# The differential-attention loop of a two-layer diffusion trunk: scores before transposes, maxima before low parts, exponentials between high parts

## The reference, cut to what matters

```python
def diff_attention(q, k, v, lam, subln_g, lam_init):
    """q (B,H,Tq,2,dk), k (B,H,Tk,2,dk), v (B,H,Tk,dv) -> (B,H,Tq,dv)."""
    scale = DIFF_QK_DIM ** -0.5
    def block(qb):
        s = jnp.einsum('bhqmd,bhkmd->bhmqk', qb, k).astype(F32) * scale
        p = jax.nn.softmax(s, axis=-1)
        a = (p[:, :, 0] - lam * p[:, :, 1]).astype(v.dtype)
        return jnp.einsum('bhqk,bhkd->bhqd', a, v)
    o = map_query_blocks(block, q)
    return rmsnorm(o, subln_g) * (1.0 - lam_init)
```

## Time and profile before

| | before |
|---|---|
| median of 3 runs | 2940.73 us (2940.59 to 2941.97) |
| the profiled execution | 2940.5 us |
| its span, first to last instruction | 2938.6 us |
| busy PE / DVE / ACT / POOL | 98% / 45% / 37% / 21% |
| granted TensorE clock, mean | 0.996 of full speed |

### The profile page before, as it was taken

How to read it: one execution, slowest core, us unless ns; L and a number is a source line. 1 busy time by engine, 2 the same in 40 slices (tenths; PEclk the granted TensorE clock), 3 DMA queues, 4 the chain that set the end, 5 groups by cost and what they waited for, 6 DMA issues and landing times.

```text
span 2938.6 us, 44082 instructions
## 1 busy us (share of the span) xinstructions
PE 2877.4 (98%) x18396; PEld 2756.4 (94%) x18396; DVE 1330.6 (45%) x2291; ACT 1076.5 (37%) x1947; POOL 614.0 (21%) x312
## 2 busy tenths in 40 slices
PE   6999999999999999999999999999999999999998
PEld 5999999999999999999999999999999989899997
DVE  4343443123557575446344434421146567554543
ACT  4333333221444544422343333323133444443231
POOL 0221221122221212122431221211221121211242
PEclk9999999999999999999999999999999999999999
DMA  5332224102111102254421121220211111215532
GB/s 224 102 110 82 102 90 137 67 15 78 42 47 47 48 32 94 80 203 141 133 79 65 66 82 39 94 83 22 70 41 45 44 48 47 78 51 183 165 110 94
DMA packets 84278, 248.55 MB, mean 85 GB/s; under 512 B 9201, under 2 KB 30193, under 8 KB 83057
## 3 DMA queue, kind: packets, MB, share of 16 engines
q1 hardware_dynamic: 84080, 245.74, 24.5%
HBM read 191.71 MB, written 54.00 MB: 84 GB/s over the span
## 4 chain that ended last, share of the span: by engine, by line
PE 89%; DVE 5%; ACT 2%; DMA 2%; issue 1%; SPq 1%; DVEq 0%; POOL 0%; POOLq 0%; ACTq 0%
PE ps L730 44%; PE ps L713 18%; PE ps L823 6%; PE ps L769 6%; PE ps L900 3%; PE ps L1041 3%; PE ps L1032 2%; PE ps L961 2%; PE ps L888 2%; PE ps L943 1%; DVE e L1839 1%; DVE stat L1822 1%; ACT e L1435 1%; DMA wmod<-w_mod 1%; DVE aTl L1846 1%
## 5 line engine op out<-in xcount | busy, mean ns | idle before, releaser
L730 PE MATMUL ps<-hhi,whi 128*128 128x384 f32 x2640 | 916.3, 347 | 5.7 <-DVE obuf L1854 3.3
L730 PE MATMUL ps<-hhi,wlo 128*128 128x384 f32 x2640 | 886.3, 336 | 0.0
L730 PE MATMUL ps<-hlo,whi 128*128 128x384 f32 x2640 | 884.1, 335 | 0.0
L1956 POOL TENSOR_TENSOR wlo<-wraw,whi 128x1024 fp32r<-128x1024 f32 (+1 forms) x188 | 415.8, 2212 | 2063.6 <-ACT whi L1127 2063.5
L730 PEld LDWEIGHTS ps<-hhi,whi 128*128 128x128 f32 x2640 | 500.0, 189 | 24.1 <-issue 7.3
L730 PEld LDWEIGHTS ps<-hlo,whi 128*128 128x128 f32 x2640 | 497.1, 188 | 0.9
L730 PEld LDWEIGHTS ps<-hhi,wlo 128*128 128x128 f32 x2640 | 495.9, 188 | 0.0
L1127 ACT ACTIVATE whi<-wraw 128x1024 fp32r<-128x1024 f32 (+1 forms) x188 | 174.5, 928 | 229.9 <-PE ps L713 209.3
L1444 ACT ACTIVATE aTh<-ps 128x512 fp32r<-128x512 f32 (+1 forms) x200 | 96.5, 482 | 278.4 <-PE ps L1032 278.4
L1691 DVE TENSOR_TENSOR ptl<-ps,pth 128x512 fp32r<-128x512 f32 (+1 forms) x144 | 82.1, 611 | 246.8 <-ACT pth L1301 246.6
L1822 DVE TENSOR_REDUCE stat<-ps 128x1 f32<-128x1152 f32 x144 | 176.5, 1231 | 16.9 <-PE ps L769 16.0
(11 more groups left out here) (199 smaller groups left out, 4835.8 us busy)
## 6 DMA issues: line engine op xcount, KB each, us to landing
wraw<-w_in SPq DMA_DIRECT2D x128, 512.0 KB, 4.2
gates_dram<-gst SPq DMA_DIRECT2D x48, 576.0 KB, 3.0
gth<-gates_dram SPq DMA_DIRECT2D x48, 576.0 KB, 4.9
mraw<-w_mod SPq DMA_DIRECT2D x32, 512.0 KB, 3.8
wraw<-w_branch SPq DMA_DIRECT2D x48, 256.0 KB, 2.8
bias<-rpb SPq DMA_DIRECT2D x8, 1280.0 KB, 6.0
outs_dram<-obuf SPq DMA_DIRECT2D x16, 576.0 KB, 3.9
oraw<-outs_dram SPq DMA_DIRECT2D x16, 576.0 KB, 3.8
```

The lines of the kernel that those rows point to most:

```text
L730: x = mm(ps[:, bank, 0:CH], a[:, s % 2, k, :], b[:, k, n * CH:(n + 1) * CH], start=(k == 0 and a is whi and b is hhi), stop=(k == KT - 1 a ...
L1956: g_.tensor_tensor(lo[:, 0:kt, :], wraw[:, n % 2, 0:kt, :], hi[:, 0:kt, :].bitcast(F32), ALU.subtract).then_inc(S.w_lo, 1)
```

## The change

Three streams are reordered in the steps t below 8, and no instruction is added or removed. On PE, `scores(t + 1)` goes ahead of the bank's wait and of `probs_t(t, 0)`. On DVE, each maximum of the next tile goes ahead of one low part. On ACT, the first exponential goes between the first and the second high part and the second one between the second and the third.

```diff
@@ PE
                     for t, units in enumerate(steps[1:]):
+                        if t < LT:
+                            scores(t + 1)
                         if t:
 
                             pe.wait_ge(*unit_evac(*steps[t][-1 if DF_TURN_BANK[h][t] == DF_TURN_BANK[h][t - 1] else 0]))
                         probs_t(t, 0)
-                        if t < LT:
-                            scores(t + 1)
                         if t and t % 2 == 0:
                             pe.wait_ge(S.df_o, o0 + t // 2)
@@ ACT
                         highs(t, 0)
                         if t < LT:
+                            exps(t + 1, 0)
                             highs(t, 1)
-                            exps(t + 1, 0)
+                            exps(t + 1, 1)
                             highs(t, 2)
-                            exps(t + 1, 1)
@@ DVE
                         if t < LT:
+                            maxes(t + 1, 0)
                             lows(t, 0)
-                            maxes(t + 1, 0)
+                            maxes(t + 1, 1)
                             lows(t, 1)
-                            maxes(t + 1, 1)
                             lows(t, 2)
                             scaled_e2(t + 1)
                             combined(t + 1)
```

## The result

| | before | after |
|---|---|---|
| median of 3 runs | 2940.73 us (2940.59 to 2941.97) | 2963.3 us (2960.89 to 2965.91) |
| ratio, 95% interval | | 1.0077 [1.0062, 1.0091] |
| the profiled execution | 2940.5 us | 2965.91 us |
| its span | 2938.6 us | 2964.0 us |

The change makes the kernel 0.8% slower; 2965 was forecast. From the start of head 0's first scores to the first L999 matmul behind head 3, in layer 0, it takes 1241.89 - 746.08 = 495.81 us before and 1256.41 - 749.52 = 506.89 us after: 11.1 us a layer, 22.2 for two, against 22.6 between the medians.

The account below looks back on a forecast made before the run. The prediction took the loop to be bound by PE's own stream, so only waits could change. New waits of +35.8 and +0.6 us less removed waits of 3.7, 4.4, 3.0 and 0.4 made +24.9 on 2940.5: 2965 us, range 2952 to 2971.

Parts of the forecast that it names:

- first case: Likeliest forecast: one wait of 0.4 to 0.75 us at group 1 in nearly every step; 2952 to 2971, likeliest 2965; chance 0.70.
- The new wait: PE before transpose group 1, t = 0 to 6 in 8 heads: 0.64 us a step, 56 x 0.64 = +35.8 us.
- G: Start of transpose group 0 in the new order, from which the prediction counts; group 1 was put at G + 2.12 us.
- the cover: PE's work between groups 0 and 1 in the new order: group 0 itself and 6 matmuls of a unit, 1.48 us.
- the new neighbours: On PE, transposes behind scores and unit matmuls no longer behind scores: 0.1 us a step taken either way in the bounds.
- The pieces of the chain: Group 0 to high part 0.63 us, to low part 0.63, to group 1 0.73: 1.99; with a maximum in front 2.12.
- Group 2: Third transpose group: may start at G + 4.11 us, PE comes at G + 4.13; no wait, margin 0.02.
- Rival 2: Group 2 waits as well: 0.15 us of lateness on ACT or DVE is +8; 2973, up to 2982; chance 0.15.
- The old waits: Removed PE waits: combined matrix -3.7 us, late group 1 at t = 5 -4.4, at t = 7 -3.0, three others -0.4.
- The shared port: GpSimd and VectorE share a port pair, first holds it; a rotation takes 3.24 us, not 1.23, during POOL's split.
- rival 3: POOL's split holds DVE's combination instead of the rotation, up to 2.0 us later: 4 x 2.0 = +8, 2973; chance 0.03.
- The sum: Whole kernel: 35.8 + 0.6 - 3.7 - 4.4 - 3.0 - 0.4 = +24.9 us on 2940.5, giving 2965.

## Why the prediction was right

The time came out 1.7 us below the forecast, by its first case. Point by point:

- **The new wait.** 0.64 us in 56 steps were forecast. Group 1 comes at G + 2.12 as worked out; what was mis-sized is the cover, 1.48 forecast and 1.56 in step 1 (result section), so that the wait is 0.56 to 0.59. The 1.48 was read behind group 1 of the kernel before, transposes that follow a unit without a gap; there the next unit starts 0.35 us after them, behind the scores 0.41 (774.26 - 773.85). The 17 steps of layer 0 with no other wait before or after became 0.54 to 0.64 us longer, 0.58 in the mean. The forecast took 0.1 either way for the new neighbours on PE; the first term came out 56 x 0.06 = 3.4 us too large.
- **The pieces of the chain.** The sum was right, because the maximum decides: 0.11 + 1.28 from group 0 to the low part (0.12 + 1.27 forecast), then 0.73. The way through the high part was read too short. It starts 0.69 to 0.75 us after the transposes, not 0.63, so that high part and maximum let the low part go at nearly the same moment. The maximum in front, charged with 0.13 us, costs 0.05 or nothing (PE's edit alone). The longer figures stand in the kernel before as well, at the group 1 that waited (952.19 in the earlier trace rows); these are the unit and the high part behind it:

```profile
952.60 0.42 PE L730 MATMUL ps<-hhi,whi 128*128 128x384 f32 x1
...
952.88 0.60 ACT L1444 ACTIVATE aTh<-ps 128x512 fp32r<-128x512 f32 x1 [4.12 <-PE ps L1032]
```

- **Group 2.** Forecast with a margin of 0.02 us. The second low part starts at 777.30, so the bank is free at 777.30 + 0.73 = 778.03, and PE comes at 778.06, 0.18 behind the last matmul as in an unbroken row: no wait, by 0.03 us. Group 1 to group 2 takes 2.09 us (778.06 - 775.97) against 2.01 before, because the unit starts 0.42 us after a group 1 that waited and not 0.35. Rival 2 didn't happen, but with a margin this thin the rows of before could not promise that: here the forecast was also lucky.
- **The old waits.** Those for the combined matrix are gone, all 8. At t = 5 and t = 7 of head 1 group 1 comes as the timeline of PE says:

```profile
959.45 0.66 PE L1032 MATMUL ps<-ident,e 128*128 128x128 f32 x4
...
961.82 0.66 PE L1032 MATMUL ps<-ident,e 128*128 128x128 f32 x4 [0.66 <-DVE aTl L1846]
...
980.94 0.33 PE L769 MATMUL ps<-kh,qh 64*128 64x128 f32 x2
...
983.50 0.65 PE L1032 MATMUL ps<-ident,e 128*128 128x128 f32 x4 [0.35 <-DVE aTl L1846]
```

At t = 5, 2.37 us after group 0 (2.12 + 0.15 were forecast); at t = 7, 983.50 - 980.94 = 2.56 us after the step's first instruction (2.5 forecast, 3.26 before).

- **The shared port.** After step 4 of head 1, DVE's combination and rotation and POOL's split; then the same rotation in head 0, which has no split beside it:

```profile
953.66 1.42 DVE L1839 SCALAR_TENSOR_TENSOR e<-e,stat,e 128x1152 f32<-128x1152 f32 x1
...
955.17 3.34 DVE L1807 TENSOR_TENSOR qraw<-xc,xr 128x1024 f32<-128x1024 f32 x1
...
955.04 2.39 POOL L1956 TENSOR_TENSOR wlo<-wraw,whi 128x1024 fp32r<-128x1024 f32 x1 [19.53 <-ACT whi L1127]
...
824.17 1.23 DVE L1807 TENSOR_TENSOR qraw<-xc,xr 128x1024 f32<-128x1024 f32 x1
```

The rotation takes 3.34 us and ends 1.08 after the split does, as in the earlier trace rows: it still is the rotation that meets the split, not the combination, which ends at 955.08. For rival 3 the split would have to start before the combination's instruction L1839 at 953.66, and it starts 1.4 us later. The meeting is what makes DVE late at t = 5: in head 0, where the rotation takes 1.23 us, group 0 to group 1 at t = 5 measures 3.58 us before and 2.12 after, in head 1 4.67 and 2.37. The old 4 x 1.09 us and the new 4 x 0.25 hang on it. The lock that the Trainium skill (SBUF - State Buffer, "SBUF: two separate sides") describes shows in both traces.
- **The sum.** 56 x 0.58 = 32.5, 4 x 0.25 = 1.0, less the 11.5 of old waits that the prediction lists: +22.0, against 22.2 for two loops and 22.6 between the medians. The term that was mis-sized is the first, by 3 us.

Left open: whether group 1 would be free in a bank of its own. That takes the cause away without any order, but all eight banks are in use in this loop, and it wasn't tried.

## What to carry to other kernels

A block of matmuls that is moved to cover one wait stops covering another: before the move, measure what the block hides now (here high part and low part between two groups that share a bank, 2.1 us), and put other work of that length in its place. The change with 9 instead of 6 matmuls behind group 0 turns 0.8% of loss into 0.3% of gain. And orders on several engines come as a set: PE's edit alone, and each pair of the three edits, is slower than before by 0.8 to 6.8%, because a late instruction holds all that is queued behind it on its engine. ACT's edit and DVE's edit each by itself were not run.

## What the runs showed of the hardware

- Four transposes that follow a unit without a gap start the next unit 0.35 us later (in the earlier trace rows, 771.45 and the unit's first matmul at 771.80) and their high part 0.63 us later. Behind the scores it is 0.41 and 0.69 to 0.75. Behind a wait it is 0.41 and 0.69 too, also in the kernel before (952.19, 952.60 and 952.88), so the runs don't show that the scores are the cause. A cover or a chain that is to hold behind a wait is better read behind a wait.
- PE's own list of waits is short by 0.15 to 0.17 us a wait, because the modelled end of the matmul before covers it: the wait of 0.56 at group 1 stands as 0.41 there, the 1.09 of the kernel before as 0.92, and the 0.35 us or so behind the third low part not at all. The list of the weight loads has these last (19.1 us in 48 waits, above).
- Where POOL's split meets a DVE instruction with two inputs in SBUF, the one that starts first keeps its usual time. In layer 0 ten splits of either kernel meet no combination and no rotation and take 2.35 to 2.41 us. Behind a combination already under way (1.42 us, as elsewhere) the split's record is longer by most of the overlap: 3.49 us where it overlaps by 1.24 (945.57 in the earlier trace rows). A part of the rotation that starts behind the split ends 1.08 us after it: it takes 3.24 to 3.48 us and not 1.23 where it starts early in the split, 1.40 where the split has 0.32 us left.
- The launch's start differs from execution to execution. The granted clock of TensorE in the stretch 30 to 45 us, by the table of stretches (busy times, then PEclk, DMA share and GB/s), in the profiled executions of before and of after:

```profile
30.00:45.00 15.00, 7.53 (x44) 6.04 (x45) 8.94 (x17) 8.47 (x11) 1.61 (x1) 0.77 0.80 325
```

```profile
30.00:45.00 15.00, 7.60 (x36) 5.19 (x37) 6.47 (x14) 6.98 (x9) 1.54 (x1) 0.59 0.79 322
```

Part of that stretch runs at the lower of the two levels (1.2 of 2.4 GHz), for longer in the second. Taken in pieces of 2 us, the granted clock is 0.50 from 38 to 44 us before, where PE has nothing to do from 36 to 40, and from 34 to 48 us after; in both, PE has nearly nothing to do from 30 to 32. It is back at 1.00 from 46 and from 50 us on, with PE at work. The 16 matmuls of L802 lie 3.52 us on the chain instead of 1.89. The same instructions stand there in both kernels, so a difference of 3.7 us between two single executions says nothing on the change; from 100 us on the granted clock is 1.00 in both.
